# State inputs and own products of the S5 mixer between units of two projections on TensorE

## The reference

```python
u_lru, u_s5, qkv_ret, q_nsa, kv_nsa, bg_nsa, gate_paths, merge = split_columns(proj, IN_SIZES)
...
x_re = jnp.einsum('bsgc,gpc->bsgp', uf, bb_re)
x_im = jnp.einsum('bsgc,gpc->bsgp', uf, bb_im)
...
_, _, h_re, h_im = lax.associative_scan(op, (a_re, a_im, x_re, x_im), axis=1)
y = (jnp.einsum('bsgp,gcp->bsgc', h_re, c_re) - jnp.einsum('bsgp,gcp->bsgc', h_im, c_im))
y = y.reshape(bsz, s, w) + d_skip * u
...
ys = ys * jax.nn.silu(gate_paths.reshape(bsz, s, N_BRANCH, BRANCH_W))
```

## Time and profile before

| what | value |
|---|---|
| median of 3 runs | 763.61 us (762.98 to 764.16) |
| time of the profiled execution | 762.22 us |
| its span in the profile | 760.4 us |
| PE busy | 740.1 us, 97% of the span |
| granted TensorE clock, mean | 0.997 |

### The profile page before, as it was taken

One profiled execution on the slowest core, in us unless ns is written; L12 is line 12 of the kernel. 1 busy time (PEld: TensorE's weight loads), 2 busy tenths in 40 slices (PEclk: granted clock), 3 DMA queues, 4 the chain that ended last, 5 costly groups with the idle time before them and its releaser, 6 DMA issues.

```text
span 760.4 us, 14637 instructions
## 1 busy us (share of the span) xinstructions
PE 740.1 (97%) x6046; PEld 630.6 (83%) x6046; DVE 486.6 (64%) x773; ACT 418.8 (55%) x673; POOL 304.3 (40%) x135
## 2 busy tenths in 40 slices
PE   7999899999999999999999998999999999999996
PEld 7888789889888888878898887888898788888785
DVE  4989977583679453534778898576564966153344
ACT  6686624546653656455458664354465546655441
POOL 3000000005778976788200000000555989766740
PEclk9999999999999999999999999999999999999999
DMA  8559464564355545555545775466635456545541
GB/s 257 149 168 283 157 224 145 176 235 139 92 157 166 169 140 166 169 164 167 147 97 167 254 189 191 144 217 194 193 98 152 136 149 186 164 135 175 170 135 55
DMA packets 87009, 126.85 MB, mean 167 GB/s; under 512 B 22072, under 2 KB 32672, under 8 KB 86944
## 3 DMA queue, kind: packets, MB, share of 16 engines
q1 hardware_dynamic: 86768, 125.89, 55.0%
q10 hardware_dynamic: 176, 0.04, 0.0%
HBM read 124.86 MB, written 1.05 MB: 166 GB/s over the span
## 4 chain that ended last, share of the span: by engine, by line
PE 85%; issue 7%; POOL 4%; DVE 1%; ACT 1%; ACTq 0%; POOLq 0%; DVEq 0%
PE proj L1695 62%; POOL w_lo L685 4%; PE M L1690 4%; PE proj L1732 4%; PE proj L1736 2%; PE M L2078 2%; PE proj L1763 2%; PE M L1883 1%; PE M L1894 1%; PE M L1851 1%; PE proj L1769 1%; PE proj L1785 1%; PE M L2052 1%; PE M L1955 1%; PE M L2047 1%
## 5 line engine op out<-in xcount | busy, mean ns | idle before, releaser
L685 POOL TENSOR_TENSOR w_lo<-raw,w_hi 128x1024 fp32r<-128x1024 f32 x112 | 287.9, 2601 | 408.4 <-ACT w_hi L707 385.3
L707 ACT ACTIVATE w_hi<-raw 128x1024 fp32r<-128x1024 f32 x200 | 206.5, 1054 | 111.9 <-PE proj L1695 64.7
L1695 PE MATMUL proj<-w_hi,h_hi 128*128 128x512 f32 x544 | 216.4, 398 | 1.5 <-POOL w_lo L685 1.5
L1695 PE MATMUL proj<-w_hi,h_lo 128*128 128x512 f32 x544 | 212.2, 390 | 0.0
L1695 PE MATMUL proj<-w_lo,h_hi 128*128 128x512 f32 x544 | 211.9, 389 | 0.0
L1695 PEld LDWEIGHTS proj<-w_hi,h_hi 128*128 128x128 f32 x544 | 102.2, 188 | 24.3 <-issue 2.7
L1695 PEld LDWEIGHTS proj<-w_hi,h_lo 128*128 128x128 f32 x544 | 102.1, 188 | 21.7
L1695 PEld LDWEIGHTS proj<-w_lo,h_hi 128*128 128x128 f32 x544 | 102.2, 188 | 20.4 <-issue 0.5
L1282 DVE TENSOR_TENSOR w_lo<-raw,w_hi 128x1024 fp32r<-128x1024 f32 x80 | 95.0, 1221 | 33.2 <-ACT w_hi L707 32.8
L1695 PE MATMUL proj<-w_hi,ys_hi 128*128 128x512 f32 x128 | 50.9, 397 | 0.5 <-POOL w_lo L685 0.5
L1695 PE MATMUL proj<-w_hi,ys_lo 128*128 128x512 f32 x128 | 50.0, 390 | 0.0
(11 more groups left out here) (335 smaller groups left out, 1200.5 us busy)
## 6 DMA issues: line engine op xcount, KB each, us to landing
raw<-in_w_in SPq DMA_DIRECT2D x152, 512.0 KB, 4.2
raw<-in_w_branch SPq DMA_DIRECT2D x32, 512.0 KB, 3.9
raw<-in_w_out SPq DMA_DIRECT2D x16, 512.0 KB, 4.6
raw<-in_s_w_glu SPq DMA_DIRECT2D x8, 512.0 KB, 4.8
raw<-in_w_in SPq DMA_DIRECT2D x8, 256.0 KB, 3.1
merged<-in_nsa_ck_w SPq DMA_DIRECT2D x4, 512.0 KB, 7.1
mt<-in_nsa_ck_w SPq DMA_DIRECT2D x4, 512.0 KB, 9.0
merged<-in_nsa_cv_w SPq DMA_DIRECT2D x4, 512.0 KB, 4.5
```

Source lines behind the costliest of these rows:

```text
L685: nc.gpsimd.tensor_tensor(w_lo[:, slot(s, l), 0:n * w], raw[:, u % N_RAW, 0:n * w], w_hi[:, slot(s, l), 0:n * w].bitcast(f32), ALU.subtrac ...
L707: i = nc.scalar.activation(out_, in_, func, **kw)
L1695: last = mm(dst, left[i], right[j], start=start and n == 0, stop=stop and n == 2, skip_group_check=True)
```

## The change

Three calls of `chunk` are cut, and the two S5 steps are placed between the pieces. Nothing is added or left out: the same 3091 rows of TensorE's program stand in another order, in each layer. The streams of DVE, ACT, POOL and SP are the same.

```diff
@@ -1916,16 +1916,19 @@
                     turn_w(1, 1)
-                    chunk("nsa_kv")
+                    chunk("nsa_kv", 0)
                     state_inputs(1)
+                    chunk("nsa_kv", range(2, 3))
                     own_outputs(0)
+                    chunk("nsa_kv", range(3, 4))
                     state_outputs(0)
                     compress(0, "ck")
                     chunk("gate_s5", 0)
                     chunk_kernels(1)
                     hidden_T(0, "ck")
-                    chunk("gate_s5", 1)
+                    chunk("gate_s5", range(2, 3))
                     own_outputs(1)
+                    chunk("gate_s5", range(3, 4))
                     state_outputs(1)
```

## The result

The changed kernel takes 756.05 us (median of 6 runs, 755.42 to 756.84) against 763.57 us for the kernel before (6 runs, 762.98 to 764.85). The ratio is 0.990 with a 95% interval of 0.9883 to 0.9918: 6.3 to 8.9 us less.

The account below looks back on a forecast made before the run. TensorE, busy 97% of the span, bounds the kernel, pausing at late instruction blocks. Removed 6.37 us, less 1.2 for passages, plus 0.27 back, nets 5.4: 763.61 − 5.4 = 758.2 us; range 757.0 to 761.2 (8 in 10).

Parts of the forecast that it names:

- first layer, `nsa_kv` to gate: First layer, first place: all 2.90 us of late blocks goes, passages cost 0.4, covering unit three's wait returns 0.17.
- first layer, gate to `gate_lru`: First layer, second place: all 0.70 us lost to a late block goes, less the cost of a passage.
- second layer, `nsa_kv` to gate: Second layer, first place: all 2.77 us of late blocks goes, passages cost 0.4, covering unit three's wait returns a guessed 0.1.
- second layer, gate to `gate_lru`: Second layer, second place: nothing was lost there, so only a passage of 0.2 us is added.
- second layer, `gate_lru`: Pause two matmuls into the second layer's `gate_lru`: stays, about 1.0 us, since state outputs stand where they stood.
- The passages: Three more switches a layer between large and small tiles, 0.2 us each, 1.2 us in all; bounds 0 and 0.4 each.
- the second rival: The 1.0 us in `gate_lru` goes too, as TensorE gains 2.3 us there and VectorE less; 757.2 us, chance 0.14.
- The front's lead: TensorE's instruction front runs some 1.2 us, about 50 instructions, ahead of the engine when asking for the next block.
- Behind both loads: Rival: second layer's first-place block waits behind two loads, comes at 459.2, 1.8 us lost; 760.0 us, chance 0.14.
- the rival at 764.5: Pauses belong to places of the stream whatever surrounds them, a price for each block; nothing won, passages cost; chance 0.05.
- block that was in time became late: Rival: another block becomes late, above all the one entered within state inputs; 760.3 to 762.3 us, chance 0.07.
- Late slots: Rival: cast and low halves slip past 5 us of cover, TensorE waits at the gate, losing over 5.4 us; chance 0.02.

Follow-up runs that it names:

- the shift: 32 small useless matmuls added in TensorE's idle time at the start of the kernel before, moving every later block boundary 128 instructions earlier in the work; 757.67 us, ratio 0.9938.
- its control: 64 small useless matmuls added at the start of the kernel before, so block boundaries stand at the same places in the work again; 762.96 us, ratio 1.0004.
- the run with the loads held: The kernel before, with SyncE holding the loads of the `gate_lru` units until the layer's first state outputs are done; 760.33 us, ratio 0.9973.
- the single cut of `nsa_kv`: The kernel before with `nsa_kv` cut once: three units, state inputs, own products, fourth unit, state outputs; gate not cut; 757.13 us, ratio 0.9923.
- the gate cut of the first layer alone: The whole change, but with `gate_s5` cut in the first layer only, the second layer's gate as in the kernel before; 755.84 us, ratio 0.9905.
- the `nsa_kv` cut with a shift: The kernel before with only `nsa_kv` cut, plus 16 small matmuls at the start, a shift by 64 instructions; 757.47 us, ratio 0.9932.

## Why the prediction was right, and where it was not

**The cause.** Right, and shown by the shift and its control: TensorE's stream is fetched in blocks of 256 instructions, and where two boundaries are crossed in less time than a block takes to come, TensorE pauses. The Trainium skill's sentence that the crossing is "mostly hidden" ("Runtime: NRT & Kernel Launch", "Instruction fetch mechanics") holds for most of the 47 blocks; behind the dense steps it doesn't, and there it was worth 7 us in 760. That loads ahead of the packet make it worse was right too; they are about half of the lost time, less than the run with the loads held was expected to show.

**The terms**, each from a start in the chain to the next, before against after:

| place | forecast | measured |
|---|---|---|
| first layer, `nsa_kv` to gate | −2.90 + 0.4 − 0.17 = −2.67 | (88.16 − 68.93) − 22.02 = −2.79 |
| first layer, gate to `gate_lru` | −0.70 + 0.2 = −0.50 | (107.64 − 88.16) − 20.00 = −0.52 |
| second layer, `nsa_kv` to gate | −2.77 + 0.4 − 0.1 = −2.47 | (455.88 − 436.61) − 21.82 = −2.55 |
| second layer, gate to `gate_lru` | +0.20 | (475.35 − 455.88) − 19.30 = +0.17 |
| second layer, `gate_lru` | 0 | −1.02 |
| first layer, ahead of `nsa_kv` | 0 | 68.93 − 68.54 = +0.39 |

(22.02, 20.00, 21.82 and 19.30 are the same distances in the kernel before.) The passages cost the 0.2 us that they were put at: a unit of 12 matmuls takes 2.94 us between small tiles. The 0.39 lies ahead of the changed calls: in after the chain there goes through ScalarE, on whose copies `turn_w(1, 0)` waits for its weights, a wait at the head of a step and no late block.

```profile
60.17 1.25 ACT gate L707 x3
61.42 0.04 issue
61.47 1.09 PE M L1690 x8
```

ScalarE had waited 3.0 us for a load there. The first profile of before goes through the place without it, that of the control with 64 small matmuls and that with the loads held, both in the order of before, have it, and so have the profiles of the `nsa_kv` cut alone and of the whole change again, but not that of the single cut of `nsa_kv`. So I put it down to the execution and not to the change.

**Two terms failed**, and only both together take the time out of the range: 758.2 less 1.0 or less 1.1 would lie inside it.

**The first failed step** is "Second layer, `gate_lru`. State outputs and what follows stand where they stood, so the 1.0 stays." Their place in the stream stayed, but not the time of the load that the packet had queued behind. SyncE issued it at 476.69 before, 0.37 us ahead of the state outputs (477.06):

```profile
476.69 1.50 SPq L456 DMA_DIRECT2D raw<-in_w_in  x2
```

Now:

```profile
472.88 3.77 SPq L456 DMA_DIRECT2D raw<-in_w_in  x4
```

that is 1.18 us behind their start at 471.70. TensorE gained 5.4 us up to there and VectorE, whose low half releases the load, only 3.8, as the second rival put it. The packet of the block starts between 472.8 and 472.9 in after, 1.1 us into the state outputs, against 479.5 to 479.7 before, 2.5 us into them:

```profile
q8 instruction: 1, 0.02, 70.8%
```

The variants agree. In the `nsa_kv` cut alone and in the gate cut of the first layer alone the load is issued 0.69 and 0.61 us behind the start of the state outputs, and the pause is gone. In the gate cut alone and with the loads held it is issued 0.54 and 0.37 us ahead of it, and the pause stays; the packet then starts some 2.3 and 2.7 us into the state outputs, against 1.1 and 1.0 in the first two.

With that the sum is 6.4 us, and the time would have been forecast at 757.2. That 762.22 − 755.81 = 6.4 is what the two profiled executions show is in part luck: the five places gave 6.7 us, and the 0.39 ahead of them took some of it back.

**The second failed step**, worth the other 7.5 − 6.4 = 1.1 us, is "The median is 1.39 above that execution, so 763.61 − 5.4". The distance from profile to median was carried over as if the change left it alone; after it is 0.24. The profiles show three things that vary from one execution to the next. Late blocks are the largest, 7.39 and 9.25 us in two executions of before. The wait at `turn_w(1, 0)` is up to 0.6. And in three profiles (the whole change again, the gate cut of the first layer alone, the `nsa_kv` cut with a shift) the granted clock is 0.59 to 0.66 from 16 to 20 us, and L1769 starts at 25.1 instead of 24.6. The later work doesn't vary: from the end of the first half of the second layer's `gate_lru` to the end, all twelve profiles take 272.6 to 272.8 us. The change takes the first of the three away, which fits the spread: 7.0 us for before (23 runs) and 1.4 for the whole change (5 runs) on one chip. In the six runs each of the result it was 1.9 and 1.4. That late blocks are the whole of the 1.1 is not shown; the second comparison, 762.78 against 756.31, has 6.5 us and needs none of it.

**Slips that change nothing.** The front's lead of 1.2 us is some 65 instructions at the pace of the own products (128 in 2.31 us), not 50. Behind both loads the block would by the prediction's own terms come at 452.2 + 3.6 + 2 × 1.5 = 458.8, for 1.4 us lost and not 1.8. And the rival at 764.5 is 0.9 above before, inside the 1.5 us of no change, so it belongs to "within" and "slower: 0.06" is too high.

**The rivals.** Waiting behind both loads in the second layer didn't happen. No block that was in time became late. Late slots cost nothing: no piece in the chain waits for a low half there.

## What to carry to other kernels

When the engine that bounds a kernel pauses in the middle of a step without a wait, count its instructions between such pauses: equal counts point to the fetch. Some useless instructions early in the stream, where the engine is idle anyway, are a cheap test of it (32 small products here; 64 held up the real work by 1.1 us). The cure is to leave a block the time to come, here some 3.5 us from one boundary to the next with idle queues and more behind loads, that is, to mix dense steps of short products with wide ones; shifting the boundaries alone can do it too, but finds other dense places. And where the profile of one execution lies well off the median, ask what varies before the distance is carried to the forecast.

## What was not expected of the hardware

In one profile of before a pause of 2.65 us was followed by two windows of 2 us at a granted clock of 0.50 and 0.71, which cost 1.1 us in one half of the gate and 0.4 in `compress`; after 2.25 and 2.29 us in the first profile of the same kernel, and after 2.50 in that of the control, it stayed at 1.00. So a late block can cost more than the pause itself. It was seen in one of three profiles with a pause of over 2.2 us, and what decides it is open.

Two late blocks in a row cost more than one, because the second is asked for only when the first is entered: with the loads held, 3.45 us from entry to entry, for 256 instructions that took 1.27 + 1.57 = 2.84 us.
